# A one-core transformer block on Trainium2: attention's small products rewritten (forget sums with 128 rows, cumulative sums from high and low parts, the gate's weights in one operand)

## What is computed

```python
h = rmsnorm(x, g_attn[l])
proj = jnp.einsum('bsd,de->bse', h, w_in[l])          # q, k, v of 16 heads, and 8 columns for the forget gate
f_logit = proj[..., o1:] + b_f[l]
log_f = jnp.transpose(jax.nn.log_sigmoid(f_logit), (0, 2, 1))

# stick-breaking heads, causal: s < t
log_beta = jax.nn.log_sigmoid(z)
log_keep = jnp.where(causal, jax.nn.log_sigmoid(-z), 0.0)
rest = lax.cumsum(log_keep, axis=3, reverse=True) - log_keep
a = jnp.where(causal, jnp.exp(log_beta + rest), 0.0)

# forgetting heads, causal: s <= t
c = lax.cumsum(log_f, axis=2)
z = z + c[:, :, i * Q_BLOCK:end, None] - c[:, :, None, :end]
p = jax.nn.softmax(jnp.where(causal, z, -jnp.inf), axis=-1)
```

## Time and profile before

| | |
|---|---|
| median of 3 runs | 2092.01 us (2089.69 to 2092.39) |
| span of the profiled execution | 2087.8 us |
| PE busy | 2028.6 us, 97% |
| PE weight loads busy | 1640.5 us, 79% |
| DVE busy | 1283.5 us, 61% |
| ACT busy | 1038.6 us, 50% |
| mean granted clock of PE | 0.992 |

### The profile page before, as it was taken

The page is one execution under the profiler, slowest core; times in us unless marked ns, Lnnn a source line. Parts: engine busy times, 40 slices in busy tenths (PEclk is TensorE's granted clock), DMA queues, the critical chain, the costliest instruction groups (busy, mean ns, idle before and its releaser), DMA issues.

```text
span 2087.8 us, 23169 instructions
## 1 busy us (share of the span) xinstructions
PE 2028.6 (97%) x8907; PEld 1640.5 (79%) x8907; DVE 1283.5 (61%) x1313; ACT 1038.6 (50%) x1369; POOL 112.9 (5%) x215
## 2 busy tenths in 40 slices
PE   3999899999999999999999999999999999999998
PEld 1777568888888888887788888888888888888887
DVE  7989877666665555557556656655555555554555
ACT  3333435445444544554666755555444544544544
POOL 0000012001101100100100100000000000000000
PEclk9899999999999999999999999999999999999999
DMA  9999998768766656754556555556665665656663
GB/s 399 410 378 373 350 355 280 284 230 287 266 227 198 223 187 201 222 197 161 181 181 203 182 173 170 182 182 208 217 200 182 238 200 182 238 197 194 208 216 120
DMA packets 225782, 484.39 MB, mean 232 GB/s; under 512 B 17648, under 2 KB 32432, under 8 KB 216848
## 3 DMA queue, kind: packets, MB, share of 16 engines
q1 hardware_dynamic: 217552, 469.56, 66.0%
q0 software_dynamic: 6960, 9.97, 1.7%
q10 hardware_dynamic: 1168, 3.46, 0.4%
HBM read 459.84 MB, written 2.10 MB: 221 GB/s over the span
## 4 chain that ended last, share of the span: by engine, by line
PE 89%; DMA 6%; DVE 4%; ACT 1%; issue 0%; ACTq 0%; DVEq 0%
PE ps L544 27%; PE ps L545 27%; PE ps L546 27%; DMA raw<-in_fnet_w 3%; DMA raw<-in_w_mlp_in 2%; DVE w_low L1409 2%; PE ps L709 2%; DMA raw<-in_w_mod 1%; DVE scr L1421 1%; DVE scr L1436 1%; ACT w_high L986 1%; PE ps L733 1%; PE ps L735 1%; PE ps L599 1%; PE ps L616 0%; PE ps L640 0%
## 5 line engine op out<-in xcount | busy, mean ns | idle before, releaser
L1409 DVE TENSOR_TENSOR w_low<-raw,w_high 128x1024 fp32r<-128x1024 f32 x672 | 818.3, 1222 | 682.0 <-ACT w_high L986 681.9
L986 ACT ACTIVATE w_high<-raw 128x1024 fp32r<-128x1024 f32 x672 | 707.4, 1058 | 875.2 <-PE ps L546 767.8
L544 PE MATMUL ps<-w_high,h_both 128*128 128x512 f32 x1536 | 605.9, 394 | 9.5 <-DVE w_low L1409 7.8
L546 PE MATMUL ps<-w_high,h_both 128*128 128x512 f32 x1536 | 599.3, 390 | 0.0
L545 PE MATMUL ps<-w_low,h_both 128*128 128x512 f32 x1536 | 599.3, 390 | 0.0
L544 PE MATMUL ps<-w_high,u_high 128*128 128x512 f32 x1152 | 449.5, 390 | 0.7 <-DVE u_low L1895 0.7
L546 PE MATMUL ps<-w_high,u_low 128*128 128x512 f32 x1152 | 448.3, 389 | 0.0
L545 PE MATMUL ps<-w_low,u_high 128*128 128x512 f32 x1152 | 448.2, 389 | 0.0
L544 PEld LDWEIGHTS ps<-w_high,h_both 128*128 128x128 f32 x1536 | 289.2, 188 | 75.2 <-DVE w_low L1409 8.5
L546 PEld LDWEIGHTS ps<-w_high,h_both 128*128 128x128 f32 x1536 | 289.1, 188 | 60.7
L545 PEld LDWEIGHTS ps<-w_low,h_both 128*128 128x128 f32 x1536 | 289.3, 188 | 60.2 <-issue 1.4
(11 more groups left out here) (195 smaller groups left out, 893.1 us busy)
## 6 DMA issues: line engine op xcount, KB each, us to landing
raw<-in_w_mod SPq DMA_DIRECT2D x96, 1024.0 KB, 7.5
raw<-in_w_mlp_in SPq DMA_DIRECT2D x64, 1024.0 KB, 5.8
raw<-in_w_mlp_out SPq DMA_DIRECT2D x64, 1024.0 KB, 5.2
raw<-in_w_up SPq DMA_DIRECT2D x64, 1024.0 KB, 5.6
raw<-in_w_down SPq DMA_DIRECT2D x64, 1024.0 KB, 5.1
raw<-in_w_in SPq DMA_DIRECT2D x48, 1024.0 KB, 5.1
raw<-in_fnet_w SPq DMA_DIRECT2D x16, 1024.0 KB, 7.3
raw<-in_w_out SPq DMA_DIRECT2D x16, 1024.0 KB, 5.1
```

The lines of the kernel that those rows point to most:

```text
L544: eng.matmul(dst, ah, wh, start=(k == 0), stop=False)
L546: last = eng.matmul(dst, al, wh, start=False, stop=(k == KT - 1))
L986: eng.activation(w_high[:, h % LEAD, :], raw[:, slot, (h % 2) * 2 * CW:(h % 2 + 1) * 2 * CW], ACT.Copy).then_inc(high_ready, 1)
L1409: eng.tensor_tensor(w_low[:, h % LEAD, :], raw[:, slot, piece], w_high[:, h % LEAD, :].bitcast(f32), ALU.subtract).then_inc(raw_used if h ...
```

## The change

- **Forget sums.** `negc_split` and `head_rows` get 128 rows; those that hold nothing are zero. L863 and L865 then contract over 128 rows.
- **Gate.** `wf_both` holds high and low weights of a block side by side, so one matmul of 512 columns and 16 stationary columns replaces the pair. It also makes low x low. The result has 16 rows and goes by one DVE copy into `gate_rows`; four f32 matmuls with `fold` (two stacked identities) add high and low rows, and both halves, as they turn them.
- **Cumulative sums.** The matrices `sum_from` and `sum_all` are kept in fp32r. ACT rounds a head's logs (`round_logs`), DVE subtracts (`low_logs`, which signals `logs_there`), and four fp32r matmuls replace the two in f32. ACT's step stands at the position behind the one where the head's "z" stands, ahead of its `high_part`; DVE's at the same position, behind its `low_part`. The parts live in the free columns 3072 to 4095 of `scr`, one buffer for all heads, so ACT also waits for the product before (`mid_ready`).
- `forget_low` prepares the new constants, three more small operations on DVE.

```diff
@@ -204,7 +204,11 @@
         grow = sb("grow", [P, D])
+        scr_at = -(-nc.sbuf_base // 32) * 32
         scr = sb("scr", [P, 2 * D])
+        logs_split = nc.alloc_sbuf_tensor_at("logs_split", [P, 1024], f32r, offset=scr_at + 4 * 3 * TT * CW)
+        logs_high, logs_low = logs_split[:, 0:384], logs_split[:, 384:768]
+        sum_from, sum_all = logs_split[:, 768:768 + P], logs_split[:, 768 + P:768 + 2 * P]
         extra = sb("extra", [P, 1536])
...
@@ -224,8 +228,9 @@
         wf = sb("wf", [P, KT * HEADS])
-        wf_high = sb("wf_high", [P, KT * HEADS], f32r)
-        wf_low = sb("wf_low", [P, KT * HEADS], f32r)
+        wf_both = sb("wf_both", [P, KT, 2, HEADS], f32r)
+        wf_high, wf_low = wf_both[:, :, 0, :], wf_both[:, :, 1, :]
+        fold = sb("fold", [2 * HEADS, HEADS])
         bf = sb("bf", [P, TT * HEADS])
...
@@ -281,9 +286,9 @@
         ew = extra[:, 768:1536].rearrange("p (b n) -> p b n", b=2)
-        negc = sb("negc", [HEADS, SEQ])
-        negc_split = sb("negc_split", [SPLIT_ROWS, SEQ], f32r)
-        head_rows = sb("head_rows", [SPLIT_ROWS, HEADS], f32r)
+        gate_rows = extra[0:2 * HEADS, 1024:1024 + 2 * SEQ]
+        negc_split = sb("negc_split", [P, SEQ], f32r)
+        head_rows = sb("head_rows", [P, HEADS], f32r)
 
...
@@ -327,6 +332,7 @@
         fox_exp = sem("fox_exp")
+        logs_rounded, logs_there = sem("logs_rounded"), sem("logs_there")
         probs_ready = sem("probs_ready")
...
@@ -817,18 +823,18 @@
                 for k in range(KT):
-                    piece = slice(k * HEADS, (k + 1) * HEADS)
-                    both = h_both[:, k, :, :].rearrange("p e s -> p (e s)")
-                    eng.matmul(side(2)[0:HEADS, :], wf_high[:, piece], both, start=(k == 0), stop=False)
-                    last = eng.matmul(side(2)[0:HEADS, 0:SEQ], wf_low[:, piece], h_high[:, k, :],
-                                      start=False, stop=(k == KT - 1))
+                    last = eng.matmul(side(2)[0:2 * HEADS, :], wf_both[:, k, :, :].rearrange("p e n -> p (e n)"),
+                                      h_both[:, k, :, :].rearrange("p e s -> p (e s)"),
+                                      start=(k == 0), stop=(k == KT - 1))
                 last.then_inc(f_sum, 1)
...
                 for tt in range(TT):
-                    last = eng.transpose(side(3)[:, tt * HEADS:(tt + 1) * HEADS], negc[:, tt * P:(tt + 1) * P],
-                                         cst[0:HEADS, C_ID:C_ID + HEADS])
+                    for e in range(2):
+                        last = eng.matmul(side(3)[:, tt * HEADS:(tt + 1) * HEADS],
+                                          gate_rows[:, e * SEQ + tt * P:e * SEQ + (tt + 1) * P], fold[:, :],
+                                          start=(e == 0), stop=(e == 1))
                 last.then_inc(f_turned, 1)
...
@@ -858,7 +864,7 @@
                     head = GH * (g - 2) + i
-                    s_h = head_rows[:, head:head + 1].to_broadcast([SPLIT_ROWS, P])
+                    s_h = head_rows[:, head:head + 1].to_broadcast([P, P])
                     eng.matmul(bank[:, 0:P], q_h[:, 0:P], k_h[:, 0:P], start=True, stop=False)
...
@@ -875,9 +881,11 @@
                 if g < 2:
-                    eng.wait_ge(mid_in, n + 1)
-                    eng.matmul(bank[:, 0:384], cst[:, C_GE:C_GE + P], e, start=True, stop=False)
-                    eng.matmul(bank[:, P:SEQ], ones, e[:, SEQ:384], start=False, stop=True)\
+                    eng.wait_ge(logs_there, n + 1)
+                    eng.matmul(bank[:, 0:384], sum_from, logs_high, start=True, stop=False)
+                    eng.matmul(bank[:, 0:384], sum_from, logs_low, start=False, stop=False)
+                    eng.matmul(bank[:, P:SEQ], sum_all, logs_high[:, SEQ:384], start=False, stop=False)
+                    eng.matmul(bank[:, P:SEQ], sum_all, logs_low[:, SEQ:384], start=False, stop=True)\
                        .then_inc(mid_ready, 1)
...
@@ -1227,7 +1235,7 @@
                 eng.wait_ge(f_raw, 48)
-                eng.activation(wf_high[:, :], wf[:, :], ACT.Copy).then_inc(f_high, 1)
+                eng.activation(wf_high, wf[:, :].rearrange("p (k n) -> p k n", k=KT), ACT.Copy).then_inc(f_high, 1)
 
...
@@ -1306,6 +1314,17 @@
 
+            def round_logs(n):
+                eng.wait_ge(mid_in, n + 1)
+                if n:
+                    eng.wait_ge(mid_ready, n)
+                eng.activation(logs_high, ew[:, n % 2, :], ACT.Copy).then_inc(logs_rounded, 1)
+
+            def logs_behind(g, jobs):
+                for job, i in jobs:
+                    if job == "z" and g < 2:
+                        round_logs(GH * g + i)
+
             def take_middle(g, i):
...
@@ -1340,6 +1359,8 @@
                         gain_updated(4 + hh)
+                    if g:
+                        logs_behind(g - 1, SLOTS.get(r * HALVES + hh - 1, ()))
                     high_part()
...
@@ -1744,13 +1765,18 @@
                 eng.wait_ge(f_high, 1)
-                eng.tensor_tensor(wf_low[:, :], wf[:, :], wf_high[:, :].bitcast(f32), ALU.subtract)\
-                   .then_inc(f_low, 1)
+                eng.tensor_tensor(wf_low, wf[:, :].rearrange("p (k n) -> p k n", k=KT), wf_high.bitcast(f32),
+                                  ALU.subtract).then_inc(f_low, 1)
+                eng.tensor_tensor(fold[:, :], ident[0:2 * HEADS, 0:HEADS], ident[0:2 * HEADS, HEADS:2 * HEADS],
+                                  ALU.add)
 
             forget_low()
+            eng.tensor_copy(sum_from, cst[:, C_GE:C_GE + P])
+            eng.tensor_copy(sum_all, ones)
             eng.tensor_copy(head_rows[0:LOW_ROW, :], ident[0:LOW_ROW, 0:HEADS])
-            eng.tensor_copy(head_rows[LOW_ROW:SPLIT_ROWS, :], ident[LOW_ROW:SPLIT_ROWS, LOW_ROW:SPLIT_ROWS])
-            link(eng.tensor_scalar(negc_split[0:LOW_ROW, :], cst[0:LOW_ROW, 0:SEQ], 0.0, None, ALU.mult))
+            eng.tensor_copy(head_rows[LOW_ROW:2 * LOW_ROW, :], ident[LOW_ROW:2 * LOW_ROW, LOW_ROW:SPLIT_ROWS])
+            eng.tensor_copy(head_rows[2 * LOW_ROW:P, :], ident[2 * LOW_ROW:P, 0:HEADS])
+            link(eng.tensor_scalar(negc_split[:, :], cst[:, 0:SEQ], 0.0, None, ALU.mult))
             eng.wait_ge(mod_cols, G2 + 1)
...
@@ -1785,9 +1811,7 @@
                 eng.wait_ge(f_sum, 1)
-                link(eng.tensor_copy(negc[:, :], side(2)[0:HEADS, 0:SEQ]))
-                eng.tensor_tensor(negc[:, :], side(2)[0:HEADS, SEQ:2 * SEQ], negc[:, :], ALU.add)\
-                   .then_inc(f_rows, 1)
+                eng.tensor_copy(gate_rows, side(2)[0:2 * HEADS, :]).then_inc(f_rows, 1)
 
...
@@ -1847,6 +1871,16 @@
 
+            def low_logs(n):
+                eng.wait_ge(logs_rounded, n + 1)
+                eng.tensor_tensor(logs_low, ew[:, n % 2, :], logs_high.bitcast(f32), ALU.subtract)\
+                   .then_inc(logs_there, 1)
+
+            def logs_behind(g, jobs):
+                for job, i in jobs:
+                    if job == "z" and g < 2:
+                        low_logs(GH * g + i)
+
             def take_middle(g, i):
...
```

## The result

The changed kernel takes 2095.4 us, the kernel before 2089.3 (medians of 12 runs each). The ratio is 1.0030, with a 95% interval of 1.0021 to 1.0039: 6.3 us slower, 4.4 to 8.1 by the interval. The profiled spans are 2093.1 against 2087.8 us. The forecast was +6.75 us on a level of 2092.0, which gave 2098.8; the level measured here is 2.7 lower, and that is most of the 3.4 between 2098.8 and 2095.4.

The account below looks back on a forecast made before the run. PE was taken to bound the kernel. Waits 11.0 + clock 1.7 - forget rows 4.7 - gate products 1.9 + turning the gate 0.65 = +6.75 us on 2092.0, giving 2098.8 us; range 2093 to 2104.

Parts of the forecast that it names:

- What bounds the kernel: PE sets the end in the attention heads: a microsecond taken from its matmuls, or waited, is one of the span.
- Forget rows: Forgetting heads: with 128 rows weight loads run ahead again, 1.09 instead of 1.83 us a head; 4.7 us kept.
- Gate products: Gate: single products replace 16 pairs, 3.65 instead of 5.57 us, gain 1.9; turning the gate loses 0.65.
- Cumulative sums: Stick-breaking heads: PE waits for DVE's subtraction behind the next low part; 11 us lost, the 2.4 gain already taken off.
- The clock: Granted clock falls behind long waits in the stick-breaking heads; one fall taken for the two groups, 1.7 us lost.
- rival (b): Clock falls after both fourth stick-breaking heads, little absorbed: +3.4 to +6.8 instead of 1.7, 2100.5 to 2103.9 us; chance 0.15.
- Rival (a): Stick-breaking heads: waits but no clock loss, +5.05, 2097.1 us; chance 0.22.
- Rival (c): Stick-breaking heads: the low part of the logs is there when PE comes, -8.35, 2083.7 us; chance 0.11.
- Rival (d): Forgetting heads: 128 rows remove no hole, it belongs to changing f32 to fp32r and back; +11.45, 2103.5 us; chance 0.07.
- The sum: Whole kernel: all terms together give +6.75 us, time 2098.8 us; chance 0.45.

Follow-up runs that it names:

- f32_sums: Changed kernel with the stick-breaking heads' middle product back in f32, straight behind the DVE sum: 2082.83 against 2088.78 us for the kernel before, ratio 0.9972.
- subtract_first: Changed kernel with DVE's subtraction moved ahead of the next half's low part: 2088.82 against 2088.78 us for the kernel before, ratio 0.9999.
- rows128_only: Kernel before with only the 128 rows in negc_split and head_rows: 2085.00 against 2088.45 us, ratio 0.9982.
- logs_on_dve: Changed kernel, but DVE rounds and subtracts right behind its sum, without ACT: 2080.93 against 2088.78 us for the kernel before, ratio 0.9969.
- high_before_low: As logs_on_dve, with PE making the high part's products once rounded and the low ones behind: 2079.89 against 2088.45 us for the kernel before, ratio 0.9968.
- changed_again: Changed kernel run once more, unedited: 2096.48 against 2088.45 us for the kernel before, ratio 1.0036.
- fill_fourth: Changed kernel with nine thrown-away products ahead of the wait at every fourth stick-breaking head: 2093.82 against 2088.78 us for the kernel before, ratio 1.0036.
- fill_first_and_fourth: Changed kernel with nine thrown-away products ahead of the waits at first and fourth stick-breaking heads: 2093.69 against 2088.45 us for the kernel before, ratio 1.0025.

## Why the prediction was right

**What bounds the kernel.** Right. What PE was made to wait, it did not get back: the stick-breaking stretch moves with the waits (f32_sums, subtract_first, the filled kernel), and the stretches behind it stay as they were (forgetting 90.4, rest 772.7 to 772.8).

**Forget rows.** Right. 1.12 us a head (forecast 1.09), loads ahead again. The later wait in the last group is there, 0.8 us behind an ACT copy (forecast 1.1). The other forgetting group shows no wait, as assumed. Kept: 4.5 (forecast 4.7), so 5.3 gross, 0.66 a head rather than 0.72. rows128_only shows that it is this part alone.

**Gate products.** Right. 3.68 us (forecast 3.65). The gate stretch fell by 1.15, the forecast was 1.9 - 0.65 = 1.25; turning the rows takes 0.99 us (1017.00 to 1017.99) instead of 0.21, a loss of 0.78 and not 0.65. The small DVE steps ahead of the gate, four and not the three of the prediction, cost nothing that shows beside the 2.6 us by which one kernel's first stretch differs from itself.

**Cumulative sums.** Right in mechanism and in order, a little too high in size. Shift after the first head: from the first score product to the first dense product behind the sums are 7.55 us before (starts 1069.85 and 1077.40) and 10.16 after (1066.03 and 1076.19), so +2.6, as forecast. The forecast's waits go from start to start. Measured so (the step to the first of the sums' products, less what it was before), forecast and measured in the first group are 2.9 and 2.75, 0.2 and 0.19, 0.6 and 0.44, 2.85 and 2.70. The first and the last are short mostly by the chain from sum to subtraction, 3.2 us and not 3.4. In brackets a trace shows less, 2.59, nothing, 0.28 and 2.54, so the 13 us of idle forecast for the two groups are 10.9 there. Two groups: 10.4 without the clock (forecast 11.0). The gain a product, forecast 0.30, is 0.30 where PE doesn't wait for it (logs_on_dve, high_before_low) and 0.2 behind a wait (at the first head 1.10 to 0.91 from the first of the products to the second dense one). High_before_low gains 1.7 and not 2.4 in the stretch because the two first heads gain nothing.

**The clock.** The mechanism was right, the term too small in the profiled execution: 3.1 us (13.5 - 10.4) where 1.7 was forecast. What was off is the count, one fourth head of two. There it fell at both, 4 x (1 - 0.57) = 1.7 us each, as much as worked out from the earlier trace rows, 3.4 by that count and 3.1 by the stretches. In that execution rival (b) is what happened, at its lower price of 3.4. In the other execution it fell at both first heads and cost 1.9, since part of it is absorbed by heads 1 to 3, as argued. Rival (b)'s condition, a fall behind the fourth heads, does not hold there. In time, where both were timed together, the changed kernel is 2.8 us slower than the filled one, between the forecast's 1.7 and rival (b)'s 3.4 and over; with so few times neither is excluded. What decides whether a wait of 2.5 us is followed by a fall isn't settled: it came behind 5 of the 8 waits of 2.5 to 2.7 us in the three profiles that have them (two of four in the changed kernel, both in changed_again, one of two in fill_fourth). So choosing one fall at the fourth heads was a guess, and that it gave the time to 0.5 us is in part luck.

**Rival (a)**, waits and no clock loss, is +5.05: fill_first_and_fourth is just that, made on purpose, and gives +5.2 in time and -1.1 + 10.4 - 4.5 = +4.8 in the stretches. Rival (a)'s time lies within the interval of the changed kernel; what speaks against it are the falls in both profiles, and the 2.8 us between the two kernels timed together. **Rival (c)**, the parts of the logs there in time, was priced at -8.35. It did not happen in the changed kernel, but its mechanism is right: when the steps are put in DVE's idle stretch, as the rival says, high_before_low is 6.7 us faster than before by the ratio and 1.1 + 1.7 + 4.5 = 7.3 by the stretches. **Rival (d)** fell with rows128_only.

**The sum.** Forecast 11.0 + 1.7 - 4.7 - 1.9 + 0.65 = 6.75; stretches 10.4 + 3.1 - 4.5 - 1.1 = 7.9 in one execution, 10.4 + 1.9 - 4.5 - 1.1 = 6.7 in the other, 6.3 in time (4.4 to 8.1). In the first, 0.6 too much for the waits stands against 1.4 too little for the clock.

## What to carry to other kernels

When a step is added between two engines, what it costs depends on the place it gets in each queue, and not only on its own length: here 1.1 us of added work delayed its reader by 3.2 to 4.3, because it stood behind work of the next half and of the head before, and moving one instruction of each head by one place gave back 9.5 us. Before a product is made cheaper on the engine that sets the pace, check that its operands are not already just in time, and let the order begin with what is ready first. A small fp32r product with 40 to 64 rows between wide ones is worth padding with zero rows, if the operands are at hand.

## What the runs showed of the hardware

- The hole around a narrow fp32r matmul is as long with 64 rows as with 40 (1.84 and 1.83 us for the head), and absent with 96 and 128 (1.12). I had only 8 and 40 to go by.
- The granted clock after a wait of one length is not the same from execution to execution: behind 2.5 to 2.7 us it fell to a mean of 0.57 to 0.62 over 4 to 8 us in 5 of 8 cases, and stayed at 1.00 in the others; behind 2.08, 2.07, 1.90 and 1.89 us it stayed. Behind the 1.94 us of the earlier trace rows it fell, so the length of the wait alone does not separate the cases.
- The 1000 us before the gate took 996.9 to 1002.5 us over all kernels and differed by 2.6 us for one of them, and the 773 us at the end took 772.7 to 772.8. One pair of profiled spans could have been wrong by several us about an effect of 6; the stretches around the edit were not.
